# Half products for tiles 4 and 5 of both feed-forward layers, with input sums shared out over three engines and the second layer's weight sums moved

## What is computed

```
def _conv_ffn(x, buf, w_up, conv_w, conv_b, w_down):
    u, v = jnp.split(x @ w_up, 2, axis=-1)
    uc, new_buf = _causal_dwconv(u, buf, conv_w, conv_b)   
    h = jax.nn.gelu(uc.astype(jnp.float32)) * v.astype(jnp.float32)
    return h.astype(x.dtype) @ w_down, new_buf.astype(buf.dtype)
```

## Time and profile before

| | |
|---|---|
| median of 3 runs | 1386.44 us (1385.7 to 1386.45) |
| profiled execution | 1385.61 us, span 1383.8 us |
| TensorE busy | 98%, 9860 matmuls |
| VectorE, ScalarE, GpSimd busy | 69%, 52%, 10% |
| granted TensorE clock, mean | 0.997 |
| DMA | 217 MB, of it 76 MB on GpSimd's queue |

### The profile page before, as it was taken

The page is one execution under the profiler, slowest core; times in us unless marked ns, Lnnn a source line. Parts: engine busy times, 40 slices in busy tenths (PEclk is TensorE's granted clock), DMA queues, the critical chain, the costliest instruction groups (busy, mean ns, idle before and its releaser), DMA issues.

```text
span 1383.8 us, 24827 instructions
## 1 busy us (share of the span) xinstructions
PE 1355.9 (98%) x9860; PEld 1328.8 (96%) x9860; DVE 956.1 (69%) x1499; ACT 718.7 (52%) x1129; POOL 137.7 (10%) x146
## 2 busy tenths in 40 slices
PE   7999999999999999999999999999999999999996
PEld 7999999999999999899999999999999999999996
DVE  5657565665778557753886778888884588458865
ACT  5443544453565345632764577755752467236734
POOL 0020111100330000000000230021400000000002
PEclk9999999999999999999999999999999999999998
DMA  8265687859749899995555221223123455335512
GB/s 312 62 230 186 139 201 194 235 111 289 208 166 210 246 264 259 274 255 140 161 160 167 76 63 61 77 62 107 47 80 92 126 161 177 97 115 161 168 62 85
DMA packets 80900, 217.47 MB, mean 157 GB/s; under 512 B 6929, under 2 KB 9233, under 8 KB 80529
## 3 DMA queue, kind: packets, MB, share of 16 engines
q1 hardware_dynamic: 52704, 138.95, 30.6%
q0 software_dynamic: 27648, 76.03, 22.9%
q10 hardware_dynamic: 432, 0.91, 0.2%
HBM read 208.23 MB, written 74.74 MB: 204 GB/s over the span
## 4 chain that ended last, share of the span: by engine, by line
PE 81%; DVE 8%; DMA 6%; ACT 4%; issue 2%; SPq 0%; DVEq 0%; ACTq 0%
PE PS L782 24%; PE PS L783 24%; PE PS L784 24%; DMA raw<-weights 4%; DMA raw<-weight_sums 2%; PE PS L951 1%; DVE wlo L1599 1%; PE PS L960 1%; DVE Y L1892 1%; PE PS L966 1%; PE PS L910 1%; DVE Y L1880 1%; PE PS L931 1%; ACT whi L1131 1%; DVE S L2221 1%
## 5 line engine op out<-in xcount | busy, mean ns | idle before, releaser
L782 PE MATMUL PS<-xhi,whi 128*128 128x296 f32 (+1 forms) x1536 | 470.3, 306 | 7.9 <-DVE wlo L1605 7.6
L783 PE MATMUL PS<-xlo,whi 128*128 128x296 f32 (+1 forms) x1536 | 458.7, 299 | 0.0
L784 PE MATMUL PS<-xhi,wlo 128*128 128x296 f32 (+1 forms) x1536 | 458.3, 298 | 0.0
L1131 ACT ACTIVATE whi<-raw 128x1024 fp32r<-128x1024 f32 (+2 forms) x256 | 253.4, 993 | 205.8 <-PE PS L784 181.2
L1599 DVE TENSOR_TENSOR wlo<-raw,whi 128x1024 fp32r<-128x1024 f32 (+2 forms) x256 | 294.1, 1152 | 74.5 <-ACT whi L1131 65.2
L782 PEld LDWEIGHTS PS<-xhi,whi 128*128 128x128 f32 x1536 | 290.8, 189 | 11.4 <-issue 8.1
L783 PEld LDWEIGHTS PS<-xlo,whi 128*128 128x128 f32 x1536 | 291.3, 190 | 1.4
L784 PEld LDWEIGHTS PS<-xhi,wlo 128*128 128x128 f32 x1536 | 290.3, 189 | 0.0
L782 PE MATMUL PS<-hhi,whi 128*128 128x296 f32 (+2 forms) x864 | 258.1, 299 | 0.4 <-DVE Y L1817 0.4
L783 PE MATMUL PS<-hlo,whi 128*128 128x296 f32 (+2 forms) x864 | 256.9, 297 | 0.0
L784 PE MATMUL PS<-hhi,wlo 128*128 128x296 f32 (+2 forms) x864 | 256.2, 297 | 0.0
(11 more groups left out here) (268 smaller groups left out, 1672.7 us busy)
## 6 DMA issues: line engine op xcount, KB each, us to landing
raw<-weights SPq DMA_DIRECT2D x118, 512.0 KB, 4.2
weight_sums<-weights POOLq DMA_DIRECT2D x24, 2048.0 KB, 16.9
raw<-weights SPq DMA_DIRECT2D x100, 256.0 KB, 3.8
weight_sums<-weight_sums POOLq DMA_DIRECT2D x8, 2048.0 KB, 12.0
raw<-weight_sums SPq DMA_DIRECT2D x64, 256.0 KB, 3.5
raw<-weight_sums SPq DMA_DIRECT2D x32, 512.0 KB, 4.2
raw<-weights SPq DMA_DIRECT2D x16, 384.0 KB, 3.1
Y<-xT SPq DMA_DIRECT2D x8, 296.0 KB, 10.5
```

What stands on the lines that cost most here:

```text
L782: pe.matmul(dst, wh, h, start=first, stop=False, skip_group_check=onto)
L783: pe.matmul(dst, wh, lo, start=False, stop=False, skip_group_check=onto)
L784: return pe.matmul(dst, wl, h, start=False, stop=last, skip_group_check=onto)
L1131: act.activation(high(u, i)[:, 0:n], raw_of(u, i), ACT.Copy).then_inc(w_hi, 1)
```

## The change

SINGLE goes from 6 to 4: tiles 4 and 5 of each layer become a pair block, and with it

- the sums form three groups a layer (2, 8 and 8 pairs; `GROUP_OF`). Layer 0's three are made in the first mixer; layer 1's first two, interleaved, behind the second LayerNorm; its third behind the third LayerNorm;
- input sums are made in tiles 0 to 3 and wait in two sets of rows by turns (`SUM_ROWS`). GpSimd makes t1 and t3 (`input_differences`), behind its rows of the LayerNorm; VectorE t2 and t4. ScalarE rounds them ahead of the tile's GELU instead of behind it;
- in single tiles too ScalarE applies the first tap.

```diff
-SINGLE = 6
+SINGLE = 4
@@
+GROUP_OF = [layer * len(GROUPS) + FFN[u - base][2] for layer, base in enumerate((U_FFN0, U_FFN1))
+            for u in PAIRS if base <= u < base + N_FFN]
@@
+        SUM_ROWS = ((KEPT, MORE), (6, 7))
@@
-                sp.wait_ge(w_sums[n // PER_GROUP], 16 * len(SUM_STEPS))
+                sp.wait_ge(w_sums[GROUP_OF[n]], 16 * len(SUM_STEPS))
@@
+            def input_differences(layer, k):
+
+                w, at = wid(U_FFN1 if layer else U_FFN0), off(U_FFN1 if layer else U_FFN0)
+                pool.wait_ge(ln_x, (4 * layer + 2) * KT)
+                if k > 1:
+                    pool.wait_ge(xt_lo, KT * layer + 2 * k - 2)
+                x11, x12, x22 = Y[:, k, span(0, at)], Y[:, k, span(1, at)], Y[:, KT // 2 + k, span(1, at)]
+                t1, t3 = (columns_of(row, w)[:, 0, :] for row in SUM_ROWS[k % 2])
+                pool.tensor_tensor(t1, x11, x12, ALU.subtract).then_inc(xt_diff, 1)
+                pool.tensor_tensor(t3, x22, x12, ALU.subtract).then_inc(xt_diff, 1)
@@
-                for group in range(2):
+                for group in range(len(GROUPS)):
                     sum_step(group, n)
@@
                 if ln == 0:
-                    for group in range(2, 4):
-                        for step in range(len(SUM_STEPS)):
+                    for k in range(KT // 2):
+                        input_differences(0, k)
+                elif ln == 1:
+                    for step in range(len(SUM_STEPS)):
+                        for group in (3, 4):
                             sum_step(group, step)
+                else:
+                    for k in range(KT // 2):
+                        input_differences(1, k)
+                    for step in range(len(SUM_STEPS)):
+                        sum_step(5, step)
@@
-                        done(act.activation(out_small("fc_p", jj * (FW - 1), FW - 1), r[:, NP:NP + FW - 1], ACT.Copy))
-                        done(act.activation(batches(out_small("fc_s", jj * NB * (FW - 1), NB * (FW - 1))),
-                                            tail[:, :, NS:], ACT.Copy))
+                        first_tap(j)
                     elif kind == "v":
+                        input_sums_hi(j)
                         smooth(j)
-                        if 1 <= j <= KT // 2:
-                            input_sums_hi(j - 1)
@@
-                    done(tt(t1, x[0][0], x[0][1], ALU.subtract))
+                    dve.wait_ge(xt_diff, KT * layer + 2 * k + 2)
                     done(stt(t2, t1, -1.0, x[1][1], ALU.mult, ALU.subtract), xt_sum)
-                    done(tt(t3, x[1][1], x[0][1], ALU.subtract))
@@
-                        done(ts(y, r[:, 0:n], par("ffn_conv_w", (layer * FW) * FT + j),
-                                par("ffn_conv_b", layer * FT + j), ALU.mult, ALU.add))
-                        for q in range(1, FW):
-                            done(stt(y, r[:, q:q + n], par("ffn_conv_w", (layer * FW + q) * FT + j), y,
-                                     ALU.mult, ALU.add), conv if q == FW - 1 else None)
+                        later_taps(j)
@@
-                        if 1 <= j <= KT // 2:
-                            input_sums_lo(j - 1)
+                        input_sums_lo(j)
```

More of the change, by code:

```diff
@@ L433, in trunk @@
         pads = sem("pads_ready")
-        w_sums = [sem(f"weight_sums_of_group{i}") for i in range(2 * (len(GROUPS) - 1))]
+        w_sums = [sem(f"weight_sums_of_group{i}") for i in range(2 * len(GROUPS))]
         h_made = sem("h_of_pair_made")
@@ L438, in trunk @@
         xt_sum, xt_hi, xt_lo = sem("input_sums_made"), sem("input_sums_hi"), sem("input_sums_lo")
+        xt_diff = sem("input_differences_made")
         tapped = sem("first_tap_done")
@@ L688, in sum_step @@
                 first, last = slice(0, HALF), slice(HALF, 2 * HALF)
-                n = group * PER_GROUP
-                units = weights[PAIRS[n]:PAIRS[n] + 2 * PER_GROUP].rearrange("(n t) p c -> t p n c", t=2)
-                sums = W_SUMS[n:n + PER_GROUP].rearrange("n p c -> p n c")
+                n, count = GROUP_OF.index(group), GROUP_OF.count(group)
+                units = weights[PAIRS[n]:PAIRS[n] + 2 * count].rearrange("(n t) p c -> t p n c", t=2)
+                sums = W_SUMS[n:n + count].rearrange("n p c -> p n c")
                 to, source, add = SUM_STEPS[step]
@@ L1370, in block_of_pairs @@
                     keep_product(n, 0)
-                    if j > first:
+                    if j > max(first, SINGLE):
                         high_of_h(j - 2, first)
                     keep_product(n, 1)
-                    if j > first:
+                    if j > max(first, SINGLE):
                         high_of_h(j - 1, first)
@@ L1951, in input_sums @@
                     x = [[Y[:, KT // 2 * low_rows + k, span(t, at)] for t in range(2)] for low_rows in range(2)]
-                    (t1, t2), (t3, t4) = ([columns_of(row, w)[:, c, :] for c in range(2)] for row in (KEPT, MORE))
-                    done(tt(t1, x[0][0], x[0][1], ALU.subtract))
+                    (t1, t2), (t3, t4) = ([columns_of(row, w)[:, c, :] for c in range(2)] for row in SUM_ROWS[k % 2])
+                    dve.wait_ge(xt_diff, KT * layer + 2 * k + 2)
                     done(stt(t2, t1, -1.0, x[1][1], ALU.mult, ALU.subtract), xt_sum)
-                    done(tt(t3, x[1][1], x[0][1], ALU.subtract))
                     done(stt(t4, t2, -1.0, x[1][0], ALU.mult, ALU.subtract), xt_sum)
@@ L2059, in later_taps @@
                 def later_taps(j):
-                    dve.wait_ge(tapped, layer * (FT - SINGLE) + j - SINGLE + 1)
+                    dve.wait_ge(tapped, layer * FT + j + 1)
                     r, y = S[:, j % 2, at:], S[:, 2 + j % 2, at:FU - FW + 1]
@@ L2105, in ffn @@
                             lambda_rows()
-                    if kind == "u" and 1 <= j <= KT // 2:
-                        input_sums(j - 1)
+                    if kind == "u":
+                        input_sums(j)
             def lambda_rows():
```

13 lines of the change are left out of this document (4 added, 9 removed).

## The result

The changed kernel is slower: 1394.84 us (median of four runs, 1392.63 to 1395.23) against 1386.07 for the kernel before on the same chip (1384.88 to 1386.45); the ratio is 1.0061, with a 95% interval of 1.0044 to 1.0079. I had written 1382.7 with a range up to 1388.5, so this lies outside. Every ratio here leaves out runs more than 1.5% above the fastest of the same kernel, which is one run of the study, the longest of experiment 3.

The account below looks back on a forecast made before the run. TensorE was taken as the bound, with weight loads binding in layer 0's second feed-forward group. The terms -6.5 - 7.1 + 6.3 + 2.6 + 1.0 = -3.7 us gave 1382.7 us, range 1377 to 1388.5.

Parts of the forecast that it names:

- the sums in the heads, costed at 0: First mixer: layer 0's own sums grow by a quarter of a 2 MB transfer in eight steps, hidden by GpSimd's idle time.
- Pairs, -6.5: Tiles 4 and 5, both layers: four units of 192 matmuls become two pairs of 168, -6.5 us on TensorE.
- Layer 1's sums leave layer 0, -7.1: Layer 0's second feed-forward group: without layer 1's sums, three windows regain 52 matmuls, -7.1 us.
- `u` 2 and `v` 2, +6.3: Tiles 0 and 1, both layers: input sums lengthen the chain, so TensorE waits at these units; +6.3 us, bounds 0 and 10.
- The fourth input row, +2.6: Sums made in `u` 3 and `v` 3 delay the first pair: +1.2 us in layer 0, +1.4 in layer 1, bounds 0 and 5.
- GpSimd's differences, 0: Feed-forward start: GpSimd's four differences of 0.82 us each end by 399.2, when VectorE still waits for the tap; cost 0.
- the 1.4 forecast in layer 0: Layer 0's `u` 2: TensorE, wanting to start at 407.0, waits 1.4 us for the last copy of `u` 1 at 408.4.
- the rival in which the differences collide: Two GpSimd differences a layer meet VectorE's two-input instructions: +2.0 to 3.3 us, 1384.7 to 1386; chance 0.05.
- GpSimd's queue in the recurrent mixer, hidden: Recurrent mixer: sixteen transfers issued from 810.9, rows of x back by 933 to 937, hidden with 4 us to spare.
- Layer 1's contention, +1.0: Layer 1's feed-forward: its last eight transfers slow the first pair and second group, between 0 and 4.8 us, taken as +1.0.
- GpSimd's queue late in the recurrent mixer: Rival: small transfers add up to 5 us each, seven rounds take 130 us and more; at 136, 1392.7 us; chance 0.08.

Follow-up runs that it names:

- experiment 3: The kernel before, plus a third transfer of 0.5 MB in every head into DRAM that nothing reads: 1389.69 us median (1382.42 to 1403.96), ratio 1.0036.
- experiment 1: The changed kernel, with the weight sums of layer 0's new first group not issued in heads 2 and 3: 1383.95 us, ratio to the kernel before 1.0014.
- experiment 2: The changed kernel, with layer 0's new first group of weight sums kept out of heads 2, 3 and 7: 1381.94 us, ratio to the kernel before 0.9993.
- experiment 8: As experiment 2, with VectorE's first copy of the states in head 5 made 12 times: 1390.95 us, ratio to the kernel before 1.0057.
- experiment 4: The kernel before, with only layer 1's weight sums moved, behind the second and third LayerNorm: 1378.23 us, ratio 0.9953.
- experiment 6: As experiment 3, with 32 of the 512 columns of each row in the third transfer: 1384.45 us, ratio to the kernel before 1.0021.
- experiment 9: As experiment 2, in tiles 0 to 2 GELU ahead of ScalarE's rounding, gate products ahead of VectorE's low parts: 1376.60 us, ratio to the kernel before 0.9964.
- experiment 5: As experiment 2, with GpSimd instead of VectorE making the input sums' low parts of rows 0 to 2: 1381.22 us, ratio to the kernel before 0.9991.
- experiment 7: As experiment 2, with VectorE's first copy of the states in head 5 made 7 times: 1385.02 us, ratio to the kernel before 1.0023.
- experiment 12: The same kernel as experiment 2, timed beside the changed kernel on one chip: 1382.37 us, ratio to the kernel before 1.0000.
- experiment 10: The same kernel as experiment 4, timed beside experiment 9 on one chip: 1378.32 us, ratio to the kernel before 0.9979.
- experiment 11: The changed kernel itself, timed again beside experiment 12 on one chip: 1389.31 us (1384.70 to 1394.85), ratio to the kernel before 1.0056.

## Why the prediction was wrong, step by step

- **The step that failed: the sums in the heads, costed at 0.** "GpSimd stands idle for 17.5 us behind the last of them ... so 5 us more there costs nothing." I looked at the end of the queue only, where LayerNorm 0's work waits. Between the transfers of one head and the next stand the stores and loads of the states, and VectorE waits for each store. In the kernel before, head 4's store was in 2.3 us ahead of that (234.9 and 237.2); experiments 1, 2 and 3 show that a 0.5 MB transfer a head can use this up. A second user was missed as well: the loads of weights for mixer 0's output share the DMA engines with the sums of head 7. I had the rule in hand, since the prediction argues from a weight load that took 7.9 us beside the sums instead of 4.1, but I applied it only where sums were taken away.
- **Its price.** A standstill of 3.0 us in the heads cost 8.3 and one of 2.2 us at mixer 0's output 3.6, by the clock. A term that stands for TensorE's waiting had to reckon with that; experiment 8 gives it alone (8.4 us in the profile for a wait of 3.3).
- **Pairs, -6.5.** TensorE's count of products is what was worked out. In layer 0 the terms close: -3.3 - 7.1 + 4.7 of new gaps is -5.7, and -5.7 was measured. In layer 1 -3.2 + 4.85 is +1.65 against a measured +2.1; 0.5 stays open.
- **Layer 1's sums leave layer 0, -7.1.** Right by the trace (407.76 against 415.00 in experiment 4). By the medians it was 5.3 us on one chip and 2.7 on another. The count of 398 matmuls was read from one execution, and experiment 6's profile shows one in which the same sums cost 3.0 us: that the term came out at 7.2 holds for the execution that it was read from. The runs of the kernel before lie between 1377.7 and 1389.3, those of experiment 4 between 1377.4 and 1380.3.
- **`u` 2 and `v` 2, +6.3.** The gaps at these two (start to start, less the usual 0.14) were 2.06 and 1.63 us in layer 0 and 1.87 and 1.70 in layer 1, together 7.3: the chain from tile to tile was worked out well, 0.5 us short a layer. Those 0.5 are GpSimd's differences, in the next point but one. Experiment 9 confirms the mechanism, and shows that it was the order within the tile, not the amount of work, that cost it.
- **The fourth input row, +2.6.** 0.98 and 1.27 us, together 2.25. I had taken 1.0 of the lateness for ScalarE's being late with its copies; experiment 9, where the chain is in time and tile 3 is as it was, has a wait of 0.2 left. So this wait came mostly with the other two.
- **GpSimd's differences, 0.** Not right, though small. By the prediction's own numbers they end at 399.2 and ScalarE's tap, for which VectorE's two taps wait, at 397.69 + 0.6 + 0.9 = 399.2, so there was no margin. In the changed kernel the first of them took 1.81 us and not 0.82, since it met a low part of VectorE's, and the last ran from 411.23 to 412.06, beside the first of VectorE's taps. The taps of tile 0 and of tile 1, where no difference runs beside them:

```profile
411.22 2.38 DVE L2083 SCALAR_TENSOR_TENSOR S<-S,W 128x608 f32<-128x608 f32 x2 [2.21 <-ACT S L1360]
...
422.52 1.74 DVE L2083 SCALAR_TENSOR_TENSOR S<-S,W 128x608 f32<-128x608 f32 x2 [2.10 <-ACT S L1360]
```

  That is +0.64; in layer 1 it is +0.42 (2.13 and 1.71). Both stand in the chain to `u` 2, which came 0.66 later than the 1.4 forecast in layer 0 and 0.47 in layer 1, where the shape was to be the same. So the rival in which the differences collide was true on a small scale, on the taps and not on the low parts.
- **GpSimd's queue in the recurrent mixer, hidden.** Right: the rows of x were taken back from 932.44 to 939.96. LayerNorm 1 had ended 6.3 us late, so this is 933.7 on the prediction's scale of 933 to 937, and ScalarE rounded the weights into them at 947.90.
- **Layer 1's contention, +1.0.** From 1045 to 1185 the changed kernel's windows of 20 us count 1065 matmuls, as many as before: 0. It is real where the sums start later or TensorE is earlier (experiments 5 and 9).

Without the failed step the sum would have stood: -6.5 - 7.1 + 9.5 + 0 = -4.1 with the measured waits, -3.7 as forecast, and 9.6 - 12.0 = -2.4 in the profile, where 0.5 of layer 1's feed-forward and 0.6 each of the mixer and of the end are not accounted for. The kernel that has all of the change but not that step, experiment 2, took 1381.94 and 1382.37 us on its chips. Against the kernel before there, it is level (0.9993 and 1.0000), and not 0.3% faster. The likely reason is that the kernel before lost less to its sums in most of those runs than in the profiled one, as experiment 6's profile shows to be possible; it was not itself profiled on those chips, so this stays open.

No rival of mine was this one. The nearest, GpSimd's queue late in the recurrent mixer, had a transfer more lengthen each round of GpSimd's queue by up to 5 us, which is what it did, but at the other of the two places where the change adds them; and it gave landing as the reason and not bytes, while experiment 6 speaks for bytes.

## What to carry over

When transfers are added to a queue, go through every instruction that stands between them, not only what stands at the end: here each head's state store sat behind the sums, 2 us from being waited for. Where a margin is that small, the time becomes a matter of the execution, and one profile shows one outcome. And order within an engine is worth trying ahead of moving work to another: two swapped lines took away all of the new waits, which three of four low parts on GpSimd did not.

## What the hardware showed

- The granted clock fell to 0.50 for about 10 us behind a standstill of 3.2 to 3.3 us in the heads (TensorE's idle time), twice with different causes (the changed kernel, experiment 8), and for 3.4 us behind one of 2.2 us at 363. It stayed at 1.00 behind 1.6 us at 238 (experiment 7), behind 2.1 us at 569 in the kernel before and, in experiment 3, behind 2.8 us at 585 between the pairs:

```profile
585.00:589.00 4.00, 1.21 (x9) 1.00 1.10 268
589.00:593.00 4.00, 4.00 (x31) 1.00 0.87 309
```

  Even the same wait of the same kernel went both ways. Behind the 1.9 us at `u` 2 in layer 0 the clock stayed up in experiment 2 (first row) and fell for 3.4 us in experiment 12 (second row):

```profile
409.00:412.40 3.40, 3.40 (x27) 1.00 0.01 2
...
410.60:413.90 3.30, 3.30 (x15) 0.50 0.00 0
```

  It cost nothing there, since the 1.5 us that TensorE would have waited at `v` 2 went in exchange: the feed-forward is 409.27 and 409.29 us long. A wait in the recurrent mixer also went both ways, in experiments 4 and 10, which are one kernel: the clock fell behind a wait of 1.9 us at 896 in the first and not behind one of 1.7 in the second, and there it cost: the mixer took 179.08 and 177.25 us. Which standstill is followed by the lower clock can't be read from its length, and no run of this study separates what else decides. The Trainium skill (TensorE: Matmul & The Clock Gate, Part 1: The HAM clock gate) has an idle TensorE at 1.2 GHz and a busy one at 2.4. The trace agrees in the heads and at 363, and the row at 589 shows a TensorE that had stood idle and did not fall back.
- In the first mixer a 2 MB transfer that GpSimd issues while an earlier one is under way stood for some 15 to 25 us ahead of its issue, with no releaser in the profile. In head 3 that was 15.5 to 18.5 us in ten profiles, 18.3 to 21.4 with 0.5 MB more ahead of it, and 16.2 with 1/16 of those bytes. The stores of the states behind it (512 and 64 KB) were in 5.4 us after they were issued in the kernel before, 17 us behind the transfer's issue, and 11.5 in the changed kernel, 6 us behind it; in experiment 11 it was 6.9 us, 10 behind it.
- A row of low parts (128x592, two inputs) takes VectorE 0.79 us (experiment 2) and GpSimd 1.82 (experiment 5).
